# Merged prompt and decode attention: the new keys' scores two steps earlier, and the decode scores ahead of the prompt's scores on TensorE

## Chip, cores and metric

The kernel runs on one core of one Trainium2 chip. The metric is the device time of one execution in microseconds (us), the median of several runs.

## What is computed

One step of a hybrid causal decoder layer, for a prompt of 1024 tokens and for 8 decode sequences ("batches" below) of 8 tokens each, which have 4096 earlier tokens in a paged cache (32 pages of 128 tokens per batch). Of the layer only the differential attention matters here. There are 4 heads, each with two query/key sub-heads of 64 dims and a value of 128 dims; the rest of the layer (projections, gated linear attention, output projection, FFN, embedding) stands ahead of it and behind it.

```python
def diff_attend_prompt(q, k, v, lam):
    ...
        s = jnp.einsum('bqhcd,bkhcd->bhcqk', qi, k).astype(F32) * scale
        ...
        s = jnp.where(kpos[None, :] <= qpos[:, None], s, -jnp.inf)
        a = jax.nn.softmax(s, axis=-1)
        w = a[:, :, 0] - lam * a[:, :, 1]
        return jnp.einsum('bhqk,bkhv->bqhv', w.astype(v.dtype), v)
    ...

def diff_attend_sample(q, k, v, lam, k_past, v_past):
    ...
    s_past = jnp.einsum('bqhcd,bkhcd->bhcqk', q, k_past).astype(F32) * scale
    s_new = jnp.einsum('bqhcd,bkhcd->bhcqk', q, k).astype(F32) * scale
    s_new = jnp.where(jnp.tril(jnp.ones((T, T), dtype=bool)), s_new, -jnp.inf)
    a = jax.nn.softmax(jnp.concatenate([s_past, s_new], axis=-1), axis=-1)
    w = (a[:, :, 0] - lam * a[:, :, 1]).astype(v.dtype)
    return (jnp.einsum('bhqk,bkhv->bqhv', w[..., :P], v_past)
            + jnp.einsum('bhqk,bkhv->bqhv', w[..., P:], v))
```

## The kernel before, in words

`attention` (from line 1179) runs both attentions in one loop, written out by hand for each engine as a list of instructions with semaphore waits. The loop variable is t, with STEPS = 74 steps. Nothing reorders the lists: what stands first on an engine is issued first, and a wait holds everything behind it on that engine.

- Decode. A step t below NKV = 64 takes one group of 4 cache pages (512 past keys); NG = 8 groups make a batch. TensorE turns the keys of the 4 heads (`turn_keys`, L1425, 4 transposes a head), ScalarE copies heads 0 to 2 out of PSUM (`take_keys`, L1320), VectorE head 3 (L1588). One step later `score(t - 1)` (L1437) multiplies them with the batch's queries into the one bank S_BANK. VectorE takes the maximum (`max_scores`, L1593) and copies the scores to SBUF (`copy_scores`, L1599) in the step after that, and `score` waits for the copy of the scores before it (`s_taken`). LAG = 9 steps after its keys a group is exponentiated (`exps`, L1331, on ScalarE), its probabilities are turned (`turn_p`, L1460), copied by VectorE (`take_p`, L1627) and multiplied with the values (`values`, L1479).
- The end of a batch. `score_new` (L1447) gives the scores of the batch's 8 new tokens; `take_new` on VectorE adds their mask (L1609), takes their maximum (L1611), then the maximum over the batch (L1613) and its negative (L1615), on which the batch's exponentials wait. A second exponential (L1336) covers the new keys; its probabilities are turned by `turn_new_p` (L1454).
- Prompt. A unit is one head and one block of 128 queries, 32 units in the order of `UNITS` (1, 8, 2, 7, 3, 6, 4 and 5 blocks of keys, by turns), two steps each, one for each sub-head: `prompt_scores(t)` (L1389) on TensorE, then `prompt_maxima(t)` on VectorE (mask add L1548, maximum L1550, negative L1552), then the exponential on ScalarE in step t + 1 (`prompt_exps`, L1296). There is one pair of score banks, so `prompt_scores(t)` waits for the exponential of t - 1 (`exp_done`). In even steps VectorE also combines the two sub-heads of the unit before (`prompt_combine`, L1560 to L1565) ahead of the mask add; TensorE turns and multiplies the result (L1402, L1409).
- The ring. Turned keys, turned probabilities, the new keys' scores and the merged output of a batch share three PSUM banks in turn. `Ring` numbers the uses in TensorE's order, and `emptied(key)` waits until the use three places earlier has been copied away by its owner, ScalarE (`ring_act`) or VectorE (`ring_dve`).

SyncE loads the key pages, four steps ahead (a slot is free when its keys have been turned), and GpSimd the value pages, four steps ahead (free when `values` is done).

TensorE's order within a step is: turned keys 0 and 1; the prompt's product (even steps) or its turn (odd); turned keys 2 and 3; merge; turned new probabilities; turned probabilities; second part of the prompt's turn; `prompt_scores(t)`; `score(t - 1)`; `score_new`; `values`. VectorE's is: `finalize`, `max_scores(t - 2)`, `take_new`, `copy_scores(t - 2)`, `take_keys(t, 3)`, `take_new_p`, `take_p`, the combine, `prompt_maxima(t)`, the next batch's queries, `final_scale`. In the kernel before, `score_new` of batch b stands in step 8b + 8 and `take_new` in step 8b + 9.

Of the kernel before, what the change touches and what calls it, by code (L numbers as in the profile page):

```python
# [15 lines left out]
ALU = mybir.AluOpType  # L16
ACT = mybir.ActivationFunctionType
AX = mybir.AxisListType
# [5 lines left out]
DB, DS = 8, 8  # L24
# [1070 lines left out]
NG = NPG // 4  # L1095
NKV = DB * NG
LAG = NG + 1
STEPS = NKV + LAG + 1
UNITS = [(h, i) for h in range(H) for i in (0, 7, 1, 6, 2, 5, 3, 4)]
NU = len(UNITS)  # L1100
# [15 lines left out]
class Ring:  # L1116
# [4 lines left out]
    def __init__(self):  # L1121
        self.index, self.emptied, self.owners = {}, {}, []
        count = {"act": 0, "dve": 0}

        def use(key, owner):
            self.index[key] = len(self.owners)
            count[owner] += 1
            self.emptied[key] = count[owner]
            self.owners.append((owner, count[owner]))

        for t in range(STEPS):
            if t < NKV:
                for h in range(H):
                    use(("keys", t, h), "act" if h < 3 else "dve")
            b, last = divmod(t - LAG - NG, NG)
            if last == 0 and 0 <= b < DB:
                use(("merge", b), "act")
            v = t - LAG
            if 0 <= v < NKV:
                if v % NG == 0:  # L1140
                    use(("new_p", v // NG), "dve")
                use(("p", v), "dve")
            b, last = divmod(t - NG, NG)
            if last == 0 and 0 <= b < DB:
                use(("new_s", b), "dve")

# [32 lines left out]
def attention(nc, io, m, ps, scr, sems):  # L1179
# [14 lines left out]
    d = {n: sems("p4_" + n) for n in names.split()}  # L1194
# [36 lines left out]
    with nc.Block() as block:  # L1231
# [143 lines left out]
        def _(pe):  # L1375
            def prompt_scores(k):
                if k >= 2 * NU:
                    return
                n, c = divmod(k, 2)
                (h, i), u = UNITS[n], UNITS[n][0] % 2  # L1380
                if n % 8 == 0 and c == 0 and h:
                    pe.wait_ge(k_in[h], 64)
                if c == 0 and n >= QR:
                    pe.wait_ge(q_in[n % QR], 32 * (n // QR))
                if k:
                    pe.wait_ge(s["exp_done"], k)
                for r in range(2):
                    rows = slice(DK * r, DK * r + DK)
                    ins = pe.matmul(score_banks[:, r, 0:shown(i) * P], m.aq[rows, n % QR, c, :],  # L1389
                                    m.ak[u][rows, c, 0:shown(i) * P], start=True, stop=True)  # L1390
                ins.then_inc(s["scored"], 1)
# [99 lines left out]
            for t in range(STEPS):  # L1491
                v = t - LAG
                n, c = divmod(t, 2)
                if t < NKV:
                    turn_keys(t, 0)
                    turn_keys(t, 1)
                if c == 0 and 0 <= n - 2 < NU:
                    prompt_out(n - 2)
                if c == 1 and 0 <= n - 1 < NU:
                    prompt_turn(n - 1, 0)  # L1500
                if t < NKV:
                    turn_keys(t, 2)
                    turn_keys(t, 3)
                if t >= LAG + NG and (t - LAG - NG) % NG == 0:
                    merge((t - LAG - NG) // NG)
                if 0 <= v < NKV:
                    if v % NG == 0:
                        turn_new_p(v // NG)
                    turn_p(v)
                if c == 1 and 0 <= n - 1 < NU and pieces_of(n - 1) == 2:  # L1510
                    prompt_turn(n - 1, 1)
                prompt_scores(t)
                if 1 <= t <= NKV:
                    score(t - 1)
                if t and t % NG == 0 and t // NG <= DB:
                    score_new(t // NG - 1)
                if 0 <= v < NKV:
                    values(v)

        @block.vector  # L1520
        def _(dve):
# [68 lines left out]
            def max_scores(k):  # L1590
                b, g = divmod(k, NG)
                dve.wait_ge(d["s_full"], k + 1)
                dve.tensor_reduce(mx[:, g:g + 1], S_BANK, AX.X, ALU.max)  # L1593

            def copy_scores(k):
                b, g = divmod(k, NG)
                if b:
                    dve.wait_ge(d["exp_done"], k - NG + 1)
                dve.tensor_copy(m.ss[:, 512 * g:512 * g + 512], S_BANK).then_inc(d["s_taken"], 1)  # L1599

            def take_new(b):

                key = ("new_s", b)
                dve.wait_ge(d["ring_filled"], ring.filled(key))
                dst = m.ss[:, PAST:PAST + NS]
                if b:
                    dve.wait_ge(d["expn_done"], b)
                a = CONST_COLS["past"][0] + 56 - b * DS
                dve.tensor_tensor(dst, ring_bank(key)[:, 0:NS], m.consts[:, a:a + NS], ALU.add).then_inc(d["ring_dve"], 1)  # L1609
                dve.wait_ge(d["ring_dve"], ring.emptied[key])  # L1610
                dve.tensor_reduce(mx[:, NG:NG + 1], dst, AX.X, ALU.max).then_inc(d["mx"], 1)  # L1611
                dve.wait_ge(d["mx"], b * 2 + 1)
                dve.tensor_reduce(ssum[:, 1:2], mx, AX.X, ALU.max).then_inc(d["mx"], 1)  # L1613
                dve.wait_ge(d["mx"], b * 2 + 2)
                dve.tensor_scalar(negm[:, b % 2:b % 2 + 1], ssum[:, 1:2], -SC, None, ALU.mult).then_inc(d["negm"], 1)  # L1615

            def take_new_p(b):
# [31 lines left out]
            queries(0)  # L1649
            for t in range(STEPS):  # L1650
                v = t - LAG
                n, c = divmod(t, 2)
                if t >= LAG + NG and (t - LAG - NG) % NG == 0:
                    finalize((t - LAG - NG) // NG)
                if 0 <= t - 2 < NKV:
                    max_scores(t - 2)
                if 0 < t - 1 <= NKV and (t - 1) % NG == 0:
                    take_new((t - 1) // NG - 1)
                if 0 <= t - 2 < NKV:
                    copy_scores(t - 2)  # L1660
                if t < NKV:
                    take_keys(t, 3)
                if 0 <= v < NKV:
                    if v % NG == 0:
                        take_new_p(v // NG)
                    take_p(v)
                if c == 0 and 0 <= n - 1 < NU:
                    prompt_combine(n - 1)
                prompt_maxima(t)
                if t % NG == 4 and t // NG + 1 < DB:  # L1670
                    queries(t // NG + 1)
                if t >= LAG + NG - 1 and (t - LAG - NG + 1) % NG == 0:
                    final_scale((t - LAG - NG + 1) // NG)
                if HALVES < t <= HALVES + H:
                    norm_prompt(t - HALVES - 1)
# [890 lines left out]
```

## Time and profile before

| | |
|---|---|
| runs before | 2042.34, 2041.23, 2040.16 us; median 2041.23 |
| profiled execution | 2040.47 us, its span 2038.8 us |
| busy share of the span | PE 91%, PEld 84%, DVE 48%, ACT 30%, POOL 19% |
| mean granted TensorE clock | 0.963 |
| attention, by the trace | from 519 us (first turned keys) to about 945 us (last values) |

PE is TensorE's matmuls, PEld its weight loads, DVE is VectorE, ACT ScalarE, POOL GpSimd, SP SyncE. L1389 is line 1389 of the kernel before. Times in the trace count from the start of the span. A row of the timeline gives start, duration, engine, line, operation, what it writes and reads, the number of instructions and, in brackets, the engine's idle time ahead of it with what ended it. A row of the waits gives who waited for whom, the time in total, how many times, and the longest.

### The profile page before, as it was taken

To read this page: it belongs to the slowest core of one execution; us is meant where nothing else is said; L and a number is where in the kernel's file an instruction comes from. 1 tells how busy PE (TensorE), PEld (TensorE's weight loads), DVE (VectorE), ACT (ScalarE), POOL (GpSimd) and SP (SyncE) were. 2 spreads that over 40 slices of the span, in tenths; PEclk is the share of its full clock that TensorE was granted. 3 is DMA by queue.
4 is the path that set the end of the run, shared out by engine and by line. 5 is a ranking of instruction groups with operands and counts; after the bars stand their busy time and mean duration, and the time that the engine had idled before them with its cause. 6 is when DMAs were issued, how large, how long until landed. Compare 5 with 4: busy or idle time off the path is not lost. (4 is left out here: it accounts for less than half of the span.)

```text
span 2038.8 us, 35290 instructions
## 1 busy us (share of the span) xinstructions
PE 1863.9 (91%) x13412; PEld 1718.4 (84%) x13412; DVE 971.9 (48%) x1356; ACT 608.9 (30%) x1086; POOL 397.2 (19%) x393
## 2 busy tenths in 40 slices
PE   4999999575899999996999999999999999998898
PEld 4999999463566767664898999999999999998798
DVE  4223730486677777775325334344334333436443
ACT  4113321442465655563322211111111111113320
POOL 1112420232123333332112011101101110104110
PEclk9999999696899999998999999999999999999899
DMA  4332640204799999987111111111111111110221
GB/s 141 97 85 76 156 114 21 65 3 145 247 329 348 360 337 366 356 257 228 32 42 52 47 47 32 52 43 49 45 42 42 42 53 42 32 54 20 85 64 44
DMA packets 201583, 239.02 MB, mean 117 GB/s; under 512 B 15425, under 2 KB 142354, under 8 KB 201426
## 3 DMA queue, kind: packets, MB, share of 16 engines
q1 hardware_dynamic: 180946, 169.75, 27.0%
q0 software_dynamic: 20480, 67.13, 9.7%
q8 instruction: 105, 1.72, 0.4%
q14 instruction: 52, 0.43, 0.1%
HBM read 215.44 MB, written 16.91 MB: 114 GB/s over the span
## 5 line engine op out<-in xcount | busy, mean ns | idle before, releaser
L150 PE MATMUL psum<-h_hi,w_hi 128*128 128x364 f32 x1248 | 278.7, 332 | 2.8 <-issue 2.8
L150 PE MATMUL psum<-h_lo,w_hi 128*128 128x364 f32 x1248 | 276.3, 330 | 0.0
L150 PE MATMUL psum<-h_hi,w_lo 128*128 128x364 f32 x1248 | 275.2, 328 | 0.0
L2078 ACT ACTIVATE w_hi<-w_raw 128x1024 fp32r<-128x1024 f32 x66 | 68.8, 1059 | 586.3 <-PE psum L150 565.5
L150 PEld LDWEIGHTS psum<-h_hi,w_hi 128*128 128x128 f32 x1248 | 215.4, 189 | 4.9 <-issue 4.2
L150 PEld LDWEIGHTS psum<-h_lo,w_hi 128*128 128x128 f32 x1248 | 217.1, 189 | 0.0
L150 PEld LDWEIGHTS psum<-h_hi,w_lo 128*128 128x128 f32 x1248 | 216.7, 188 | 0.0
L2054 POOL TENSOR_TENSOR w_raw<-w_raw,gains 128x1024 f32<-128x1024 f32 x42 | 80.5, 1916 | 652.2 <-DMA w_raw<-in_w_ffn_gate 353.0
L1163 POOL DMA_DIRECT2D dec_v<-in_cache_v x256 | 137.5, 537 | 316.6 <-issue 316.6
L150 PE MATMUL psum<-x_hi,w_hi 128*128 128x364 f32 x792 | 188.5, 347 | 9.7 <-DVE x_lo L1911 5.8
L150 PE MATMUL psum<-x_hi,w_lo 128*128 128x364 f32 x792 | 176.5, 331 | 0.0
L150 PE MATMUL psum<-x_lo,w_hi 128*128 128x364 f32 x792 | 176.3, 331 | 0.0
L2194 DVE TENSOR_TENSOR h<-h,psum 128x1092 f32<-128x1092 f32 x88 | 113.5, 1289 | 108.0 <-PE psum L150 108.0
L150 PEld LDWEIGHTS psum<-x_hi,w_hi 128*128 128x128 f32 x792 | 137.3, 191 | 16.5 <-DVE x_lo L1911 6.3
L1425 PE MATMUL psum<-consts,dec_k 128*128 128x128 f32 x1024 | 139.7, 281 | 12.2 <-DVE dec_s L1609 6.1
L1320 ACT ACTIVATE dec_kt<-psum 128x512 f32<-128x512 f32 x192 | 108.4, 599 | 139.8 <-PE psum L1425 139.8
L1425 PEld LDWEIGHTS psum<-consts,dec_k 128*128 128x128 f32 x1024 | 115.2, 143 | 31.6 <-issue 17.0
L150 PEld LDWEIGHTS psum<-x_lo,w_hi 128*128 128x128 f32 x792 | 139.4, 190 | 0.0
L150 PEld LDWEIGHTS psum<-x_hi,w_lo 128*128 128x128 f32 x792 | 138.9, 190 | 0.0
L2173 DVE TENSOR_TENSOR t_up<-psum,rstd_and_sum 128x1092 f32<-128x1092 f32 x22 | 28.5, 1296 | 205.9 <-PE psum L150 205.9
L150 PE MATMUL psum<-hidden_hi,w_hi 128*128 128x364 f32 x528 | 116.9, 330 | 2.5 <-DVE w_lo L2164 2.5
L150 PE MATMUL psum<-hidden_lo,w_hi 128*128 128x364 f32 x528 | 117.4, 331 | 0.0
(262 smaller groups left out, 2793.4 us busy)
## 6 DMA issues: line engine op xcount, KB each, us to landing
dec_k<-in_cache_k SPq DMA_DIRECT2D x256, 256.0 KB, 5.1
dec_v<-in_cache_v POOLq DMA_DIRECT2D x256, 256.0 KB, 5.2
w_raw<-in_w_in SPq DMA_DIRECT2D x25, 512.0 KB, 3.9
w_raw<-in_w_ffn_gate SPq DMA_DIRECT2D x22, 512.0 KB, 3.9
w_raw<-in_w_ffn_up SPq DMA_DIRECT2D x22, 512.0 KB, 3.8
w_raw<-in_w_ffn_down SPq DMA_DIRECT2D x22, 512.0 KB, 3.6
feat_swap<-feat_n SPq DMA_DIRECT2D x32, 136.5 KB, 2.4
x_in<-in_x_prompt SPq DMA_DIRECT2D x4, 1024.0 KB, 8.2
```

The source lines that it names most:

```text
L150: ins = pe.matmul(out[:, c, 0:SPAN], w(k), x(k)[:, c * SPAN:c * SPAN + SPAN], start=n == 0 and w is whi and x is xhi, stop=n == len(ks) - ...
L1163: eng.dma_start(ring[:, slot, p:p + 1, :], cache[bass.ds(page, 1)].rearrange("o t f -> t o f")).then_inc(sem, 16)
L1320: act.activation(m.kt[:, t % 2, h, :], ring_bank(("keys", t, h)), ACT.Copy).then_inc(d["ring_act"], 1)
L1425: ins = pe.transpose(ring_bank(key)[:, p * P:p * P + P], m.kr[:, t % KR, p, h * P:h * P + P], ident)
L2054: gp.tensor_tensor(m.raw[:, u], m.raw[:, u], gain(m, "ffn").unsqueeze(2).broadcast_to([P, KT, P]), ALU.mult).then_inc(s["w_scaled"], 1)
L2078: act.activation(m.whi[:, slot], m.raw[:, u], ACT.Copy).then_inc(s["w_hi"], 1)
L2173: dve.tensor_tensor(spans(dst), dense[bank][:, :, 0:SPAN], spans(m.rb[:, :]), ALU.mult).then_inc(s["evacuated"], 1)
L2194: dve.tensor_tensor(spans(m.h[:, n]), spans(m.h[:, n]), dense[n % 2][:, :, 0:SPAN], ALU.add).then_inc(s["evacuated"], 1)
```

## The change

`score_new(b)` moves from step 8b + 8 to step 8b + 6 (`NEW_AT` = NG - 2), on TensorE and in the ring's numbering. On VectorE the mask add and the maximum of the new scores (`take_new`) move to step 8b + 7, behind `copy_scores`; the maximum over the batch and its negative become a function of their own, `batch_max`, which stays in step 8b + 9 between `max_scores` and `copy_scores`. And on TensorE, in every step, `score(t - 1)` stands ahead of `prompt_scores(t)`. No instruction is added or left out; the semaphore `mx` gets one more count per batch.

```diff
@@ constants and Ring
 LAG = NG + 1
+NEW_AT = NG - 2
...
-            b, last = divmod(t - NG, NG)
+            b, last = divmod(t - NEW_AT, NG)
             if last == 0 and 0 <= b < DB:
                 use(("new_s", b), "dve")
@@ TensorE
-                prompt_scores(t)
                 if 1 <= t <= NKV:
                     score(t - 1)
-                if t and t % NG == 0 and t // NG <= DB:
-                    score_new(t // NG - 1)
+                prompt_scores(t)
+                if t % NG == NEW_AT and t // NG < DB:
+                    score_new(t // NG)
                 if 0 <= v < NKV:
                     values(v)
@@ VectorE
-                dve.tensor_reduce(mx[:, g:g + 1], S_BANK, AX.X, ALU.max)
+                ins = dve.tensor_reduce(mx[:, g:g + 1], S_BANK, AX.X, ALU.max)
+                if g == NG - 1:
+                    ins.then_inc(d["mx"], 1)
...
                 dve.tensor_reduce(mx[:, NG:NG + 1], dst, AX.X, ALU.max).then_inc(d["mx"], 1)
-                dve.wait_ge(d["mx"], b * 2 + 1)
+
+            def batch_max(b):
+                dve.wait_ge(d["mx"], b * 3 + 2)
                 dve.tensor_reduce(ssum[:, 1:2], mx, AX.X, ALU.max).then_inc(d["mx"], 1)
-                dve.wait_ge(d["mx"], b * 2 + 2)
+                dve.wait_ge(d["mx"], b * 3 + 3)
                 dve.tensor_scalar(negm[:, b % 2:b % 2 + 1], ssum[:, 1:2], -SC, None, ALU.mult).then_inc(d["negm"], 1)
...
                 if 0 < t - 1 <= NKV and (t - 1) % NG == 0:
-                    take_new((t - 1) // NG - 1)
+                    batch_max((t - 1) // NG - 1)
                 if 0 <= t - 2 < NKV:
                     copy_scores(t - 2)
+                if (t - 1) % NG == NEW_AT and (t - 1) // NG < DB:
+                    take_new((t - 1) // NG)
                 if t < NKV:
                     take_keys(t, 3)
```

TensorE, from the turned probabilities of step 30 to those of step 31 (batch 3, so 8b + 6 and 8b + 7), before; `dec_p` are probabilities, `att_q` the prompt's queries, `dec_qb` the decode queries, `dec_k` the cache's keys:

```order
L1460 MATMUL psum<-consts,dec_p 128x128 x4
L1389 MATMUL psum<-att_k_97,att_q 128x384 x2
L1437 MATMUL psum<-dec_kt,dec_qb 32x512 x4
L1479 MATMUL psum<-dec_v,dec_pt 32x128 x16
L1425 MATMUL psum<-consts,dec_k 128x128 x8
L1402 MATMUL psum<-consts,att_p 128x128 x4
L1425 MATMUL psum<-consts,dec_k 128x128 x8
L1460 MATMUL psum<-consts,dec_p 128x128 x4
```

The same place in the changed kernel, whose lines stand one further on:

```order
L1461 MATMUL psum<-consts,dec_p 128x128 x4
L1438 MATMUL psum<-dec_kt,dec_qb 32x512 x4
L1390 MATMUL psum<-att_k_97,att_q 128x384 x2
L1448 MATMUL psum<-dec_new_k,dec_qb 32x64 x4
L1480 MATMUL psum<-dec_v,dec_pt 32x128 x16
L1426 MATMUL psum<-consts,dec_k 128x128 x8
L1403 MATMUL psum<-consts,att_p 128x128 x4
L1426 MATMUL psum<-consts,dec_k 128x128 x8
L1461 MATMUL psum<-consts,dec_p 128x128 x4
```

The decode scores and the prompt's scores have changed places, and the new keys' scores (`dec_new_k`) stand in this step. The second group of 8 `dec_k` transposes in step 31 begins with the third head; in the ring that head is now the third use after the new keys' scores.

VectorE in step 33 (8b + 9), from the end of the batch before to the copy of key head 3, before:

```order
L1644 TENSOR_SCALAR dec_osc<-psum,att_small 128x128
L1593 TENSOR_REDUCE att_small<-psum 128x1
L1609 TENSOR_TENSOR dec_s<-psum,consts 128x64
L1611 TENSOR_REDUCE att_small<-dec_s 128x1
L1613 TENSOR_REDUCE att_small<-att_small 128x1
L1615 TENSOR_SCALAR att_small<-att_small 128x1
L1599 COPY dec_s<-psum 128x512
L1588 COPY dec_kt<-psum 128x512
```

In the changed kernel the add on the new keys' scores and their maximum (there L1612 and L1614) stand in step 31 (8b + 7), from the maximum of the scores to the mask add of the prompt:

```order
L1594 TENSOR_REDUCE att_small<-psum 128x1
L1602 COPY dec_s<-psum 128x512
L1612 TENSOR_TENSOR dec_s<-psum,consts 128x64
L1614 TENSOR_REDUCE att_small<-dec_s 128x1
L1589 COPY dec_kt<-psum 128x512
L1632 COPY dec_pt<-psum 128x512
L1549 TENSOR_TENSOR psum<-psum,consts 128x2x128
```

They are behind the copy of the scores now; step 33 keeps the two instructions of `batch_max` between the maximum and the copy.

## Rows read from the trace of the kernel before

**Rows 1.** Windows, main stretch: length, busy time by engine, PEclk, DMA share, GB/s

```profile
600.00:650.00 50.00, 46.84 (x590) 35.14 (x589) 36.72 (x79) 29.94 (x79) 17.70 (x33) 1.00 1.03 350
```

**Rows 2.** Waits, 515 to 960 us: total, times, longest

```profile
DVE dec_kt L1588 <- PE psum L1425: 69.4, 46, 3.2
...
PE psum L1389 <- ACT att_p L1296: 11.6, 25, 1.0
...
PE psum L1425 <- DVE dec_s L1609: 6.1, 7, 1.0
...
ACT dec_p L1331 <- DVE att_small L1615: 2.6, 7, 0.9
```

**Rows 3.** Waits, 575 to 912 us, then 515 to 566 us

```profile
PE psum L1389 <- ACT att_p L1296: 7.9, 20, 0.6
...
PE psum L1389 <- ACT att_p L1296: 3.7, 5, 1.0
```

**Rows 4.** Windows, steps 3, 4, 5 and 7

```profile
536.41:541.56 5.15, 4.13 (x33) 2.29 (x29) 3.62 (x7) 2.83 (x6) 1.61 (x3) 1.00 1.05 344
541.56:545.90 4.34, 3.61 (x34) 2.41 (x30) 4.20 (x8) 3.27 (x8) 0.54 (x1) 1.00 1.06 336
545.90:550.23 4.33, 4.33 (x40) 3.04 (x36) 4.13 (x11) 3.00 (x7) 1.61 (x3) 1.00 1.05 345
...
555.97:561.22 5.25, 4.24 (x34) 2.40 (x30) 3.98 (x7) 2.94 (x6) 1.61 (x3) 1.00 1.04 366
```

**Rows 5.** Timeline, steps 3 and 4, TensorE and VectorE

```profile
540.57 1.07 PE L1437 MATMUL psum<-dec_kt,dec_qb 128*32 128x512 f32 x8
540.68 0.43 DVE L1548 TENSOR_TENSOR psum<-psum,consts 128x256 f32<-128x256 f32 x1 [1.47 <-PE psum L1389]
...
543.08 0.68 DVE L1599 COPY dec_s<-psum 128x512 f32<-128x512 f32 x1
```

**Rows 6.** Timeline, steps 30 and 31

```profile
701.40 0.92 PE L1389 MATMUL psum<-att_k,att_q 64*128 64x384 f32 x4
...
703.39 0.42 DVE L1548 TENSOR_TENSOR psum<-psum,consts 128x256 f32<-128x256 f32 x1
...
705.48 1.04 PE L1425 MATMUL psum<-consts,dec_k 128*128 128x128 f32 x8
705.51 0.68 DVE L1599 COPY dec_s<-psum 128x512 f32<-128x512 f32 x1
...
707.31 0.92 PE L1389 MATMUL psum<-att_k,att_q 64*128 64x384 f32 x4 [0.36 <-ACT att_p L1296]
```

**Rows 7.** Timeline, steps 22 and 23

```profile
650.98 1.13 PE L1389 MATMUL psum<-att_k,att_q 64*128 64x512 f32 x4
...
652.71 0.42 DVE L1548 TENSOR_TENSOR psum<-psum,consts 128x256 f32<-128x256 f32 x1
...
655.06 1.04 PE L1425 MATMUL psum<-consts,dec_k 128*128 128x128 f32 x8
655.09 0.68 DVE L1599 COPY dec_s<-psum 128x512 f32<-128x512 f32 x1
...
657.11 1.13 PE L1389 MATMUL psum<-att_k,att_q 64*128 64x512 f32 x4 [0.58 <-ACT att_p L1296]
```

**Rows 8.** Timeline, step 25 (8b + 9)

```profile
667.32 0.68 DVE L1593 TENSOR_REDUCE att_small<-psum 128x1 f32<-128x512 f32 x1
...
667.92 0.21 DVE L1609 TENSOR_TENSOR dec_s<-psum,consts 128x64 f32<-128x64 f32 x1
...
668.17 0.22 DVE L1611 TENSOR_REDUCE att_small<-dec_s 128x1 f32<-128x64 f32 x1
668.19 1.10 PE L1425 MATMUL psum<-consts,dec_k 128*128 128x128 f32 x8 [1.00 <-DVE dec_s L1609]
...
668.81 0.72 ACT L1331 ACTIVATE dec_p<-dec_s,att_small 128x512 f32<-128x512 f32 x1 [0.21 <-DVE att_small L1615]
...
670.58 0.30 PE L1454 MATMUL psum<-consts,dec_pn 128*128 128x128 f32 x1 [0.96 <-ACT dec_kt L1320]
```

## The prediction

> **What bounds the kernel now.** I read the page first, then the stretch in which the merged attention runs (about 519 to 945 us; nothing outside it is edited), by its windows, its waits and its order of time. In the main part of it TensorE is the bound: of 50 us it is busy 46.84, VectorE 36.72, ScalarE 29.94 [rows 1]. So what counts is TensorE's idle time, and only what the change takes away from it or adds to it. The waits of the stretch name two kinds that the change touches [rows 2]: TensorE's prompt scores waited 25 times for a prompt exponential, 11.6 us in all, and the third key head waited 7 times for a PSUM slot that VectorE frees with the add on the new keys' scores (L1609), 6.1 us. ScalarE waited 2.6 us in seven batch ends for the batch's negated maximum (L1615). VectorE itself waits for TensorE 46 times, 69.4 us, ahead of its key copy: that is the slack that hides small delays on it.
>
> I number a stretch's steps by the loop variable t; a batch b has steps 8b to 8b+7, and its first exponentials come in step 8b+9.
>
> **Part 1, decode scores ahead of the prompt's scores.** The instructions are the same, so only waits move. In steps 10 to 63 the old order lost 7.9 us in 20 waits [rows 3]. With the decode scores first, TensorE has about 1.0 us of work (L1437 lasts 1.07, the next group starts 1.0 after it, at 541.56 [rows 4, 5]) while the exponential ends; the longest of these waits is 0.6, so all of them go, provided that the decode scores' own input, VectorE's copy of the previous scores, is there. In step 31 this copy ended at 706.19 (705.51 + 0.68), while TensorE came to its prompt scores 0.36 ahead of 707.31, at 706.95 [rows 6]. It is there. Seven of the 20 waits lie in steps 8b+7, which part 2 prices: four of 0.36 as in step 31 [rows 6] and three of 0.58 as in step 23 [rows 7], 3.2 us. **Term 1: 7.9 - 3.2 = 4.7 us gained.** The prompt scores end 1.0 later in every step. VectorE's mask add follows the later of them and the combine of the odd unit: in step 30 scores ended at 702.32 and the mask add began at 703.39 [rows 6], so the delay is hidden; in step 22 they ended at 652.11, the mask add began at 652.71 [rows 7], so 0.44 of it comes through (652.11 + 1.0 + 0.05 - 652.71). In odd steps it comes through whole and is taken by the 69.4 us of slack.
>
> **Part 2, the new keys' scores two steps ahead.** They sit in a ring of three PSUM slots: whatever is the third entry after them waits for VectorE's add. Before, that was the third key head of step 8b+9; now it is the third key head of step 8b+7. VectorE's add is now behind the copy of the scores, not between maximum and copy. So I price the new wait from the old one: there the maximum ended at 668.00 (667.32 + 0.68), the add began 0.08 earlier, took 0.21, and TensorE went on at 668.19, that is 0.19 after the end of the instruction ahead of the add [rows 8]. In step 31 the copy ends at 706.19, so TensorE may go on at 706.38; it was there at 705.48 [rows 6]: 0.90 of new wait. In step 23 the copy ends at 655.77 (655.09 + 0.68), plus 0.44 from part 1, plus 0.19: 656.40 against 655.06 [rows 7]: 1.34. The 0.36 and 0.58 of the exponential that came behind it vanish inside it. Four steps of the first kind (15, 31, 47, 63), three of the second (23, 39, 55): 4 x 0.90 + 3 x 1.34 = 7.6, less 3.2. **Term 2: 4.4 us lost.** The trace of before does not show this wait. Its ends are none at all (the 3.2 would be gained) and the old wait of 1.00 [rows 8] plus 0.44 in all seven (10.1 - 3.2 = 6.9 lost); I keep the worked value, as it is made from rows of the same instructions.
>
> The old waits in steps 8b+9 go, 6.1 us, but nearly nothing is gained by that. Behind the third and fourth head TensorE waits again, 0.96 us, for ScalarE to copy the third head [rows 8], and ScalarE copies it only after the batch's first two exponentials, which start when the negated maximum is there. From the second key copy to that point ScalarE has no idle time except 0.21 [rows 8]. So TensorE comes 1.0 us earlier and waits 1.0 us longer. What is gained is what ScalarE gains: two VectorE instructions, 0.21 and 0.22 [rows 8], no longer lie ahead of the negated maximum, and of ScalarE's 2.6 us in seven waits [rows 2] about 0.3 each can go. **Term 3: 2.1 us gained** (ends 1.5 and 2.6). The four small matmuls move, they are not added.
>
> **Part 3, the steps ahead of the first values (2 to 8).** Here TensorE has little work: the four steps shown took 4.3 to 5.3 us [rows 4], and the old order lost 3.7 us in five waits for exponentials [rows 3]. With the new order the step becomes a closed loop through VectorE: mask add, reduction, decode maximum and copy, which took from 540.68 to 543.76 (543.08 + 0.68) [rows 5], 3.08; then about 0.06 to TensorE, decode scores 1.0, prompt scores 1.13 [rows 7], 0.05 back. That is 5.3 us for units of seven or eight blocks, where the old order ran the copy and the exponential side by side. Walking the loop step by step with these durations, step 3 takes 5.30 for 5.15, step 4 4.66 for 4.34, step 5 4.97 for 4.33, and step 7, with a new slot wait of 2.1 us, 6.28 for 5.25 [rows 4]; these four lose 2.1, the other three 0.4 together. **Term 4: 2.5 us lost**; ends: 3.7 gained, if all old waits simply go, and 3.7 lost, if each is replaced by one twice as long. The loop is made of rows of these very steps, so I take 2.5.
>
> **Sum:** -4.7 + 4.4 - 2.1 + 2.5 = +0.1 us. The profiled execution took 2040.47; the median of three is 2041.23, 0.76 above it. 2040.47 + 0.1 + 0.76 gives **2041.3 us**. Everything after the attention shifts with it and costs nothing. A measurement of this kernel tells about 0.2% (4.1 us) from no change, so the forecast is: no change. With the ends of the terms its own range is 2038 to 2044.5.
>
> **Transfers.** The main stretch moves 350 GB/s at a DMA share of 1.03 [rows 1], and a step of the early part 366 GB/s [rows 4]. So the transfers have been faster than the main stretch asks for, by 4%, and a gain of a few us in 340 asks for less than 1% more.
> The Trainium skill, "DMA: Bandwidth & Descriptors", section Specifications, gives about 358 GB/s as one core's limit to HBM; by it the main part would be at its end, and whatever the compute engines save would come back as waits for pages. The trace is against it in the one window of 366 GB/s.
>
> **Rivals.**
> A, faster: the slot of the new scores is free in time in steps 8b+7 (VectorE ahead by a microsecond). Then term 2 is a gain of 3.2, and without the wait in step 7 the early loss is 1.4: -4.7 - 3.2 - 2.1 + 1.4 = -8.6, 2032.6 us. Against it: the copy ended 0.7 after TensorE was there in both steps shown [rows 6, 7]. It needs VectorE to come a full 0.9 earlier.
> B, slower: the decode scores' 1.0 us lands whole on VectorE ahead of all seven slot waits. It decides at the point where the mask add of step 8b+6 starts with the prompt scores and not with the combine; in step 30 they would end at 703.3 and the mask add began at 703.39 [rows 6], a margin of under 0.1. If the combine came 1.0 earlier than there, each wait would be 1.9: 7 x 1.9 - 3.2 = 10.1 in place of 4.4, 2047.0 us. Against it: nothing in the change makes the combine earlier.
> C, the transfers are at their limit: terms 1 to 3 (2.4 gained) come back as waits for pages and term 4 stays, 2043.7 us. For it: the share of 1.03 [rows 1]; against it the 366 GB/s, and that no wait for a key page stands among the waits of the stretch. The rule cited above is this case.
>
> **Chances.** Forecast 0.78; A 0.08; B 0.06; C 0.08. A and B lie outside the range, C inside; with a little of the forecast's ends left out I give 2037.5 to 2045.0. Faster by over 0.2%: A and a little, 0.09. Slower by over 0.2%: B and a little, 0.07. Within: 0.84.
>
> **What would show it.** Right, if in the profile after: prompt scores wait for exponentials hardly at all; the third key head waits 0.9 to 1.4 us for the add on the new scores in steps 15, 23, 31 and so on, and about 2 in step 7; the turn of the new probabilities (L1454) waits about 1.6 in place of 0.96; steps 3 to 8 are longer, the decode scores waiting there for the copy. Wrong, if the add's wait is absent (A), if it is near 2 everywhere (B), if key turns wait for DMA (C), or if decode scores wait for the copy in the main part.

## Result: slower by 8 us, and where the time went

The changed kernel took 2048.46 us (median of five runs, 2047.73 to 2052.1) where the kernel before took 2040.37 (median of five in the same session, 2036.58 to 2042.34): a ratio of 1.0045, 95% interval 1.0033 to 1.0058. That is slower by more than 0.2%. The forecast, 2041.3 us and no change, was wrong, and the time lies above the range.

The waits of the changed kernel from 515 to 960 us (total, times, longest), to be read against [rows 2]:

```profile
PE psum L1455 <- ACT dec_kt L1321: 11.0, 6, 2.0
...
PE psum L1426 <- DVE dec_s L1612: 6.6, 8, 1.8
...
PE psum L1438 <- DVE dec_s L1602: 4.8, 6, 1.3
...
ACT dec_p L1332 <- DVE att_small L1620: 0.4, 1, 0.4
```

Line numbers have moved by one to five: L1390 is the prompt scores, L1426 the key turns, L1438 the decode scores, L1455 the turn of the new probabilities, L1480 the values, L1488 the merge; on VectorE L1602 is the copy of the decode scores and L1612 the add on the new scores. Most of what was foreseen is there. No wait of the prompt scores' matmuls for an exponential is left among these waits (11.6 us in 25 before [rows 2]), ScalarE's wait for the negated maximum is 0.4 in place of 2.6 [rows 2], and the wait for the add on the new scores stands at 6.6 us in its new place. The decode scores wait for the copy, 4.8 us, in five early steps as foreseen and once in the last, and the turned new probabilities wait 11.0 us in six batch ends (0.96 each before [rows 8]). TensorE's waits alone come out about even: -11.6 + 0.5 + 4.8 + 5.2. The lengths of the steps tell another story. Windows of the kernel before (length, busy time by engine, granted clock, DMA share, GB/s): step 6; steps 2 to 8; steps 9 to 62; step 63 to the last values; steps 25 and 29 alone:

```profile
550.23:555.97 5.74, 5.74 (x48) 3.98 (x45) 3.29 (x10) 2.74 (x8) 0.54 (x1) 1.00 1.05 341
...
532.08:565.98 33.90, 30.25 (x241) 19.21 (x238) 27.08 (x54) 20.08 (x48) 6.44 (x12) 1.00 1.03 339
565.98:904.44 338.46, 317.79 (x3957) 236.11 (x3951) 251.14 (x532) 203.50 (x522) 113.72 (x212) 1.00 1.00 342
904.44:945.38 40.94, 27.11 (x446) 19.77 (x442) 23.89 (x41) 14.03 (x39) 18.77 (x30) 0.95 0.71 217
665.67:674.32 8.65, 6.70 (x87) 4.75 (x83) 7.00 (x20) 5.21 (x14) 2.15 (x4) 1.00 1.04 374
692.24:697.73 5.49, 5.49 (x75) 4.20 (x71) 5.26 (x13) 3.70 (x9) 2.14 (x4) 1.00 1.03 380
```

The same of the changed kernel, without step 6, and with a stretch inside step 25 at the end:

```profile
533.29:570.04 36.75, 30.61 (x240) 19.22 (x238) 27.73 (x58) 20.55 (x48) 6.46 (x12) 1.00 1.03 331
570.04:915.67 345.63, 328.46 (x3961) 232.31 (x3960) 251.79 (x531) 203.53 (x522) 114.06 (x212) 0.99 0.98 333
915.67:954.79 39.12, 25.52 (x438) 18.40 (x434) 23.59 (x41) 13.94 (x39) 18.81 (x30) 1.00 0.73 224
670.57:680.76 10.19, 8.18 (x87) 5.25 (x83) 5.95 (x16) 5.21 (x14) 2.15 (x4) 0.83 1.04 370
698.66:704.29 5.63, 5.63 (x74) 4.09 (x71) 4.49 (x11) 3.71 (x9) 2.15 (x4) 1.00 1.00 375
...
675.70:679.10 3.40, 3.40 (x17) 1.41 (x17) 0.93 (x2) 1.34 (x4) 0.15 (x1) 0.50 1.05 356
```

Steps 2 to 8 are 2.85 us longer, steps 9 to 62 are 7.17 longer. (The last part is 1.82 shorter; the clock of the kernel before was low there once, 0.95 in its row, and with the order alone, at 1.00, the part took 39.05 too. The remaining -0.2 of the 8.0 between the spans lies in stretches that the change doesn't touch.) In the main part two things stand that no wait shows. Step 29 has no idle time of TensorE in either kernel (its busy time is its length), and yet it takes 5.63 for 5.49. And step 25 takes 10.19 for 8.65, at a mean granted clock of 0.83: for 3.4 us in it the clock is 0.50, that is 1.2 GHz in place of 2.4.

**The first: 0.14 us in a step.** TensorE in step 29, start, length and operation, before:

```profile
695.22 0.70 PE L1389 MATMUL psum<-att_k,att_q 64*128 64x256 f32 x4
695.86 1.07 PE L1437 MATMUL psum<-dec_kt,dec_qb 128*32 128x512 f32 x8
696.74 1.06 PE L1479 MATMUL psum<-dec_v,dec_pt 128*32 128x128 f32 x32
```

and after:

```profile
701.65 1.06 PE L1438 MATMUL psum<-dec_kt,dec_qb 128*32 128x512 f32 x8
702.65 0.70 PE L1390 MATMUL psum<-att_k,att_q 64*128 64x256 f32 x4
703.28 1.08 PE L1480 MATMUL psum<-dec_v,dec_pt 128*32 128x128 f32 x32
```

The decode scores last the same, but what follows them starts 0.88 us after their start where it is the values (695.86 to 696.74), and 1.00 after where it is the prompt scores (701.65 to 702.65). Decode scores and values use the array in the same shape, 128 rows by 32 columns; prompt scores use 64 by 128. The prompt scores' own successor starts 0.64 and 0.63 after them. So the group behind the decode scores can begin 0.12 earlier if it has their shape, and the change has put one of another shape between. The next step's keys begin 0.99 after the start of the values before, and 1.01 after the change; with that the 0.14 is nearly whole. The weight loads of the same two groups (PEld), the values before and the prompt scores after, show where the 0.12 lies:

```profile
696.31 0.13 PEld L1479 LDWEIGHTS psum<-dec_v,dec_pt 128*32 128x32 f32 x4 [0.30 <-DVE dec_pt L1627]
...
702.64 0.30 PEld L1390 LDWEIGHTS psum<-att_k,att_q 64*128 64x128 f32 x4 [0.84 <-issue]
```

The first weights of the values were loaded from 0.43 ahead of their first matmul, while the decode scores still ran; those of the prompt scores only as their matmul began. So it is in all of steps 9 to 62: 0.88 behind all 54 decode scores of the kernel before, 0.99 or 1.00 behind all 54 with the order alone, and where TensorE didn't wait, a group with the shape of the one ahead of it had its weights loaded 0.03 to 0.43 early in either of these two, a group with another shape never. No run changes the shape and nothing else. The Trainium skill, "TensorEngine Tiling (Array Packing)", section Tiling Modes (Key Properties), says that changing the tiling mode drains TensorE, while a change of tile alone doesn't. The rows agree with that: before, a step with values changes shape three times (keys to prompt scores, to decode scores, back to keys), after it four times.

**The second: the clock.** TensorE, then ScalarE, in step 25 of the changed kernel, to be read against [rows 8]:

```profile
675.31 0.30 PE L1455 MATMUL psum<-consts,dec_pn 128*128 128x128 f32 x1 [2.01 <-ACT dec_kt L1321]
...
676.90 1.94 PE L1438 MATMUL psum<-dec_kt,dec_qb 128*32 128x512 f32 x8
...
673.54 0.72 ACT L1332 ACTIVATE dec_p<-dec_s,att_small 128x512 f32<-128x512 f32 x1
...
674.60 0.57 ACT L1321 ACTIVATE dec_kt<-psum 128x512 f32<-128x512 f32 x1
```

Before, TensorE's idle time at this batch end came in two pieces, 1.00 ahead of the third key head and 0.96 ahead of the turned new probabilities, with 1.4 us of work between them [rows 8]. The first piece is gone with the slot wait, and, since ScalarE copies the third head no earlier than its exponentials allow, the second has grown to 2.01. So far this is what the prediction says. But right behind this piece the granted clock falls (at 0.50 from 675.7): the decode scores take 1.94 in place of 1.07 [rows 5]. It falls in the same way in steps 41 and 57, not in 9, 17, 33 and 49, whose pieces are 1.61 to 1.68.

### The profile page after: what moved, and what is told of

Same layout as the page of the kernel before. It is cut to its first block and busy times, and to the rows that moved or that the text cites. A ratio compares the mean times of both kernels' runs of the same rounds, so it can differ in the third digit from the quotient of the medians.

```text
span 2046.8 us, 35290 instructions
## 1 busy us (share of the span) xinstructions
PE 1872.5 (91%) x13412; PEld 1713.7 (84%) x13412; DVE 973.5 (48%) x1356; ACT 609.3 (30%) x1086; POOL 397.5 (19%) x393
## 5 line engine op out<-in xcount | busy, mean ns | idle before, releaser
L1426 PE MATMUL psum<-consts,dec_k 128*128 128x128 f32 x1024 | 139.7, 281 | 12.9 <-DVE dec_s L1612 6.6
L1426 PEld LDWEIGHTS psum<-consts,dec_k 128*128 128x128 f32 x1024 | 115.2, 143 | 29.4 <-issue 13.5
```

The lines of the kernel that those rows point to most:

```text
L1426: ins = pe.transpose(ring_bank(key)[:, p * P:p * P + P], m.kr[:, t % KR, p, h * P:h * P + P], ident)
```

## Experiments

Eleven kernels were run, each 5 to 12 times beside the kernel before (its medians in the three sessions: 2040.39, 2038.67 and 2039.84). Each has one profile, of one of these runs; what is said of idle pieces and of the clock is said of that execution.

**The two parts apart.** The first kernel is the one before with the order of the change and nothing else:

```diff
-                prompt_scores(t)
                 if 1 <= t <= NKV:
                     score(t - 1)
+                prompt_scores(t)
                 if t and t % NG == 0 and t // NG <= DB:
                     score_new(t // NG - 1)
```

> Only the decode scores ahead of the prompt's scores; the new keys' scores stay where they were. Theory (three separate causes: lost overlap, clock, slot wait): TensorE loses 0.14 us in each of the 55 steps that have values, since the prompt's scores now stand between decode scores and values (+7.7); the waits for exponentials go in the main part (-7.9); steps 2 to 8 lose about 1.9 without the slot wait in step 7; the idle time at batch ends stays in two pieces of 1 us, so the granted clock stays at its upper level there. Sum +1.7 on 2040.4: 2042. Rival (all of the loss is the new slot wait): order alone gains the 7.9 and loses 1.9: 2034. Rival (all of the loss is the order): 2048.

Measured: 2039.32 us, ratio 0.9997 (0.9988 to 1.0006). Windows of step 6, steps 9 to 62 and step 29:

```profile
552.31:558.04 5.73, 5.73 (x46) 3.97 (x44) 3.67 (x9) 2.74 (x8) 0.54 (x1) 1.00 1.05 330
...
568.66:905.50 336.84, 323.82 (x3957) 230.40 (x3952) 252.18 (x533) 203.51 (x522) 113.73 (x212) 1.00 1.00 343
...
694.38:700.01 5.63, 5.63 (x75) 4.09 (x71) 4.49 (x11) 3.70 (x9) 2.14 (x4) 1.00 1.03 377
```

Step 29 takes 5.63 here too, so the 0.14 belongs to the order. Step 6, which has no values and in which keys follow the decode scores in the old order, takes 5.73 for 5.74: no loss where one shape change is only exchanged for another. In 54 steps (9 to 62) 0.14 makes 7.6 us; the whole of these steps is 1.62 shorter, so the exponentials' waits were worth about 9.2 (an estimate from these two numbers), where their rows say 7.9 [rows 3]: a wait of 0.36 in its row was worth 0.43 of its step. That is part of why the kernel came out 2.7 below the 2042 that its own sum gave; neither rival came. The order alone gains in the main part nearly the 2.0 that it loses in steps 2 to 8.

The second kernel is the changed one with the old order:

```diff
+                prompt_scores(t)
                 if 1 <= t <= NKV:
                     score(t - 1)
-                prompt_scores(t)
```

> Only the new keys' scores two steps ahead; the prompt's scores stay ahead of the decode scores. Theory (three causes): no 0.14 per step; the third key head waits about 0.85 in steps 8b+7 in place of 0.36 or 0.58 for the exponential (+2.8); batch ends -0.3 each (-2.1); TensorE idle there in one piece of 1.6 to 2.0 us. Without a lower clock after it 2041; if the granted clock falls after some of these pieces, 1.8 us more for each, up to 2047 for three. Rival (all is the slot wait): 2048 without any low clock in the batch-end steps. Rival (all is the order): 2040.

Measured: 2046.33 us, ratio 1.0035 (1.0023 to 1.0046). The order alone costs nothing in sum; the move alone costs 5.9 of the 8 us. Its windows of step 25:

```profile
668.57:678.50 9.93, 8.03 (x87) 5.69 (x83) 6.87 (x19) 5.15 (x14) 2.15 (x4) 0.83 1.05 377
```

It has the low clock as the changed kernel has it, in steps 9, 17, 25, 41 and 49, each time behind one idle piece of 1.6 to 1.9 us.

**Is it the idle piece?** The third kernel is the changed one, with the merge's matmul, which stands just ahead of the idle piece, issued five times into the same place:

```diff
-                pe.matmul(ring_bank(("merge", b))[0:32, 0:DV], const(m, "merge"), m.osc[:, :], start=True, stop=True
-                          ).then_inc(d["ring_filled"], 1)
+                for again in range(5):
+                    ins = pe.matmul(ring_bank(("merge", b))[0:32, 0:DV], const(m, "merge"), m.osc[:, :],
+                                    start=True, stop=True)
+                ins.then_inc(d["ring_filled"], 1)
```

> The changed kernel with the small merge product issued five times instead of once into the same place (batch ends 1 to 7), so that TensorE's one idle piece of 2.0 us there is cut to about 1. Theory (clock): the granted clock no longer falls in steps 25, 41, 57, which go from 10.2 back to about 8.3 us: -5.6 on 2048.5, so 2043. Rival (the batch end is longer because of VectorE's or ScalarE's chain): steps 25, 41, 57 keep 10.2 us, 2048.5 or a little more.

Measured: 2043.07 us, ratio 1.0013 (1.0003 to 1.0023). Windows of steps 9 to 62 and of step 25:

```profile
569.66:910.60 340.94, 328.97 (x4009) 235.78 (x4007) 251.88 (x531) 203.30 (x522) 113.74 (x212) 1.00 0.99 338
...
670.19:678.81 8.62, 7.48 (x95) 5.54 (x91) 5.96 (x16) 5.20 (x14) 2.15 (x4) 1.00 1.05 370
```

More work, and the kernel is 5.4 us faster than the changed one: from step 17 on the pieces are 0.8 and 1.1 us now, the clock stays at 1.00 in all these steps, and step 25 takes 8.62 for 10.19. Steps 9 to 62 are 4.69 shorter, 1.56 for each of the three falls.

**What does the slot wait cost?** The fourth kernel is the changed one with the add on the new scores as VectorE's first work of its step, ahead of the decode maximum and copy:

```diff
+                if t and (t - 1) % NG == NEW_AT and (t - 1) // NG < DB:
+                    take_new((t - 1) // NG)
                 if 0 <= t - 2 < NKV:
                     max_scores(t - 2)
...
-                if (t - 1) % NG == NEW_AT and (t - 1) // NG < DB:
-                    take_new((t - 1) // NG)
```

> The changed kernel with VectorE's add and maximum on the new keys' scores as the first work of step 8b+7, ahead of maximum and copy of the decode scores. Theory (slot wait): the add ends before TensorE comes to the third key head, so the waits of 0.48 (steps 15, 31, 47, 63) and 0.94 (23, 39, 55) there go to under 0.2, and most of the 1.8 in step 7: -5, so 2043.5, if the granted clock falls as often as in the changed kernel. Rival (the third head is held by something else, or the time comes back at the decode scores): 2048.5.

Measured: 2039.1 us, ratio 1.0001 (0.9991 to 1.0012). In the changed kernel the add had stood here, in step 23 (VectorE's copy and add, then TensorE's third head):

```profile
659.75 0.68 DVE L1602 COPY dec_s<-psum 128x512 f32<-128x512 f32 x1
660.35 0.21 DVE L1612 TENSOR_TENSOR dec_s<-psum,consts 128x64 f32<-128x64 f32 x1
...
660.62 1.09 PE L1426 MATMUL psum<-consts,dec_k 128*128 128x128 f32 x8 [0.94 <-DVE dec_s L1612]
```

Windows of the new kernel, steps 9 to 62, 23 and 25, and TensorE in step 25:

```profile
566.27:901.91 335.64, 322.73 (x3961) 230.73 (x3959) 251.72 (x531) 203.56 (x522) 114.07 (x212) 1.00 1.01 345
...
653.89:659.58 5.69, 5.69 (x71) 3.68 (x67) 4.46 (x10) 3.64 (x8) 2.15 (x4) 1.00 1.04 366
665.00:673.70 8.70, 6.70 (x87) 4.68 (x83) 5.95 (x16) 5.21 (x14) 2.15 (x4) 1.00 1.04 376
...
669.74 0.30 PE L1455 MATMUL psum<-consts,dec_pn 128*128 128x128 f32 x1 [2.00 <-ACT dec_kt L1321]
```

Step 23 has no idle time left; it took 1.09 more in the changed kernel (658.36 to 665.14, 6.78), step 31 took 0.71 more (6.33 for 5.62). So the six slot waits of steps 9 to 62 cost some 5.4 us. The surprise is step 25: the idle piece ahead of the turned new probabilities is 2.00 us here as well, and the clock did not fall in any step of the main part of this profile. Three falls of 1.56 would be 4.7, about what the median came out below the 2043.5 expected; but the profile is the fastest of the eleven runs, and whether the others had no fall either isn't shown.

**Is the fall then due to the slot wait?** In the profiles so far, either cure had been enough. The fifth kernel is the second with the fourth's edit: the move alone, without its slot wait.

```diff
+                prompt_scores(t)
                 if 1 <= t <= NKV:
                     score(t - 1)
-                prompt_scores(t)
...
+                if t and (t - 1) % NG == NEW_AT and (t - 1) // NG < DB:
+                    take_new((t - 1) // NG)
                 if 0 <= t - 2 < NKV:
                     max_scores(t - 2)
```

> The new scores two steps ahead, their add first on VectorE, and the prompt scores ahead of the decode scores as before: the move alone without its slot wait. Theory (in the runs so far the clock fell behind a batch end only where a slot wait stood two steps ahead of it; the move is worth about 0.3 us at each of seven batch ends): no fall in the main stretch, 2037 to 2039 us. Rival (TensorE's one idle piece of 1.6 to 1.9 us is enough by itself, as in the run of the move alone with its slot wait): falls of 3.4 us behind several batch ends, 2042 to 2046 us.

Measured: 2044.62 us, ratio 1.0023 (1.0015 to 1.0032). The theory is out, the rival holds. (The profiled run was the fastest of twelve, 2039.61, by what lies ahead of the attention; from step 2 to the last values it took 418.6 us, the kernel before 413.3.) TensorE in steps 33 and 57:

```profile
717.57 0.30 PE L1455 MATMUL psum<-consts,dec_pn 128*128 128x128 f32 x1 [1.82 <-ACT dec_kt L1321]
...
719.18 1.93 PE L1438 MATMUL psum<-dec_kt,dec_qb 128*32 128x512 f32 x8
...
871.83 0.30 PE L1455 MATMUL psum<-consts,dec_pn 128*128 128x128 f32 x1 [1.90 <-ACT dec_kt L1321]
...
873.48 1.06 PE L1438 MATMUL psum<-dec_kt,dec_qb 128*32 128x512 f32 x8
```

There is no slot wait in the main part, and the clock fell in steps 17, 25, 33, 41 and 49, behind pieces of 1.81 to 1.90; behind the 1.90 of step 57 it did not.

**Does the length decide, or the moment?** Two more kernels. In the sixth, which is the third with two issues in place of five, the pieces are a little shorter than in the changed kernel:

```diff
-                for again in range(5):
+                for again in range(2):
```

> The changed kernel with the merge's matmul issued twice, the second with the same result in the same place. Theory (the length of the idle piece decides: in the changed kernel it fell behind 2.0 us and not behind 1.68 us): the pieces of steps 25, 41 and 57 come to 1.8 us; if that is short enough, no fall, 2043 us. Rival (the length is not what decides, the move alone had falls behind 1.6 to 1.9 us): three falls as in the changed kernel, 2048 us.

In the seventh, the changed kernel does some 1.7 us more work once, in step 13 (7.37 us there for 5.63), and is the same otherwise:

```diff
-                for p in range(4):
+                for p in list(range(4)) * (5 if v == 4 else 1):
                     ins = pe.transpose(ring_bank(("p", v))[:, p * P:p * P + P], m.pg[:, v % 2, p * P:p * P + P], ident)
```

> The changed kernel with the four turns of step 13 issued five times into the same place: 1.76 us more work of TensorE, once, and every later step that much later; nothing else differs. Theory (each idle piece of 2.0 us makes the clock fall, whenever it comes): again three falls, in steps 25, 41 and 57, 2050 us. Rival (it depends also on the moment at which the piece comes): the falls move to other batch ends, or one goes; 2045 to 2050 us.

Measured: 2049.45 (1.0046, 1.0031 to 1.006) and 2052.23 (1.0065, 1.0052 to 1.0078). TensorE in step 25 of the sixth kernel:

```profile
677.33 0.30 PE L1455 MATMUL psum<-consts,dec_pn 128*128 128x128 f32 x1 [1.78 <-ACT dec_kt L1321]
...
678.59 1.94 PE L1438 MATMUL psum<-dec_kt,dec_qb 128*32 128x512 f32 x8
```

and in steps 25 and 41 of the seventh:

```profile
675.87 0.30 PE L1455 MATMUL psum<-consts,dec_pn 128*128 128x128 f32 x1 [2.01 <-ACT dec_kt L1321]
...
676.88 1.07 PE L1438 MATMUL psum<-dec_kt,dec_qb 128*32 128x512 f32 x8
...
776.72 0.30 PE L1455 MATMUL psum<-consts,dec_pn 128*128 128x128 f32 x1 [2.00 <-ACT dec_kt L1321]
...
778.26 1.93 PE L1438 MATMUL psum<-dec_kt,dec_qb 128*32 128x512 f32 x8
```

1.78 us made the clock fall as 2.0 did, in steps 25, 41 and 57. In the seventh kernel the very piece that brought a fall in the changed kernel (2.01, step 25) brought none, and the same piece in steps 41 and 57 did. So the length alone doesn't decide. Over all profiles 1.61 (step 9) brought a fall in three of seven, 1.67 to 1.68 in none of nine pieces. Two falls more came in steps 7 and 9 of both kernels, which the changed kernel's profile doesn't have. Step 7 of the seventh kernel (6.21 us at 1.00 in the changed kernel):

```profile
554.44:562.29 7.85, 6.04 (x37) 2.63 (x31) 3.91 (x8) 3.05 (x6) 1.61 (x3) 0.78 0.99 340
```

These steps stand ahead of its edit: up to step 12 it is the changed kernel, instruction for instruction. So the same pieces in the same code brought a fall in one execution and none in another, and the fall that step 25 lost need not be due to the added work. The moment at which a piece comes is what is left of the two ideas, but no run sets it alone: what decides stays open. Both medians lie above what either idea gave (2048 and 2050 at most), which the two falls more would explain.

**Filling the idle piece.** If the piece is the trouble, work that is there anyway can be put into it. In the step of a batch's first values the turned probabilities are moved behind the prompt scores, first in the kernel before, then in the changed kernel (where the prompt scores already stand behind the decode scores):

```diff
-                if 0 <= v < NKV:
-                    if v % NG == 0:
-                        turn_new_p(v // NG)
+                first_group = 0 <= v < NKV and v % NG == 0
+                if 0 <= v < NKV and not first_group:
                     turn_p(v)
...
                 prompt_scores(t)
+                if first_group:
+                    turn_new_p(v // NG)
+                    turn_p(v)
```

> The kernel before, in which the first step of a batch's values turns the new exponentials and the first old ones behind the prompt scores. Theory (TensorE's idle time at the seven batch ends, 0.96 us ahead of the turned new exponentials, is a wait that other work can fill): the rows of that wait vanish, about 0.9 us x 7 = 6 us less, 2034 us, if nothing is late behind it. Rival (the turned exponentials still have to be copied before the values start, with only the 1.0 us of the decode scores between them): the wait moves to the values, 2038 to 2041 us.

> The changed kernel with the same late turns. Theory (the granted clock falls because TensorE's idle time at a batch end stands in one piece of 2.0 us): with the piece filled by prompt turns and scores the clock does not fall behind steps 25, 41 and 57 (3 x 1.8 = 5.4 us less) and up to 1 us of idle time goes in each of seven steps: 2036 to 2043 us. Rival (the fall comes from the slot wait two steps ahead, not from the idle piece): the clock still falls in those steps, 2043 to 2048 us.

Measured: 2030.23 us, ratio 0.9958 (0.9945 to 0.9971), and 2036.7 us, ratio 0.9991 (0.998 to 1.0001). TensorE in step 25 of the first, and its steps 9 to 62:

```profile
667.41 1.10 PE L1425 MATMUL psum<-consts,dec_k 128*128 128x128 f32 x8 [1.00 <-DVE dec_s L1611]
...
669.89 0.33 PE L1454 MATMUL psum<-consts,dec_pn 128*128 128x128 f32 x1
```

```profile
566.64:900.01 333.37, 318.58 (x3959) 236.12 (x3952) 250.80 (x532) 202.71 (x522) 113.71 (x212) 1.00 1.01 348
```

The wait of 0.96 ahead of the turned new probabilities is gone without a new one behind it in this step. Steps 9 to 62 are 5.1 us shorter than in the kernel before; the medians differ by 8.4, and the profile, of the slowest of the five runs, doesn't show the rest. In the changed kernel the 2.0 us piece becomes two of about 0.4, and no fall is left in steps 2 to 62:

```profile
668.69 1.06 PE L1438 MATMUL psum<-dec_kt,dec_qb 128*32 128x512 f32 x8 [0.47 <-DVE dec_s L1604]
...
671.87 1.08 PE L1480 MATMUL psum<-dec_v,dec_pt 128*32 128x128 f32 x32 [0.41 <-DVE dec_pt L1634]
```

**All of it.** The last two kernels take the new scores early, their add first on VectorE, the late turns, and the old order of the prompt scores; the second puts the decode scores first in the six steps of sixteen where the wait for the exponential was longest:

```diff
+                ahead = t > NG and t % 16 in (3, 4, 7, 8, 11, 15)
+                if ahead and t <= NKV:
+                    score(t - 1)
                 prompt_scores(t)
...
-                if 1 <= t <= NKV:
+                if 1 <= t <= NKV and not ahead:
                     score(t - 1)
```

> New scores early, their rows taken first on VectorE, prompt scores ahead of decode scores as before, late turns at a batch end. Theory (the parts add up: the lost 0.14 us per step is not paid, the slot wait is gone, the exponentials' waits are back, the idle piece is partly filled): 2032 to 2036 us. Rival (the prompt scores' waits for the exponentials come back in full and the late turns only move the wait): 2039 to 2041 us.

> As b1_best, but from step 9 on the decode scores stand ahead of the prompt scores in the six steps of sixteen whose prompt scores wait for an exponential by more than 0.14 us. Theory (a step pays 0.14 us where the decode scores stand first, and saves the wait where there is one): some 9 us of waits gone for 21 x 0.14 = 3 us lost, 5 to 6 us below b1_best. Rival (the waits come from work that falls behind elsewhere, and come back in the next step): as b1_best within 1 us.

Measured: 2029.07 us, ratio 0.9948 (0.9936 to 0.9961), and 2027.91 us, ratio 0.9948 (0.9935 to 0.996). Both beat both kernels, the first by more than was expected. Steps 9 to 62 of the first:

```profile
565.96:897.45 331.49, 317.42 (x3964) 236.35 (x3960) 250.48 (x531) 202.77 (x522) 114.08 (x212) 1.00 1.01 350
```

and of the second, where the choice takes only 2 of the expected 5 to 6 us off them, and TensorE at the start of step 41, where time came back:

```profile
566.16:895.66 329.50, 320.36 (x3964) 235.74 (x3960) 250.29 (x531) 202.79 (x522) 113.73 (x212) 0.99 1.02 352
```

```profile
761.28 1.97 PE L1426 MATMUL psum<-consts,dec_k 128*128 128x128 f32 x8 [2.72 <-DMA dec_k<-in_cache_k]
```

The steps with the decode scores first are each shorter by about the wait less 0.14, as the theory says, 5.8 us without steps 40 and 41; but ahead of step 41 a key page is late by 2.72 us, and the clock falls with that piece too (0.81 in step 41): these two steps are 3.8 longer. One profile can't tell whether this belongs to the kernel. The intervals of the two don't separate them. Nor do they separate either from the late turns alone, which take the most part of the gain with the smallest edit. Steps 9 to 62 of the second moved 352 GB/s.

## Why the prediction was wrong

The sum was +0.1 us (and 0.76 to the median); the spans differ by 8.0. Term by term, for the same stretches:

- **The step that failed: "The instructions are the same, so only waits move."** They are the same, but the spacing between two of them depends on which follow each other. The decode scores' successor starts 0.88 after them if it has their shape and 1.00 if not; in all, 0.14 a step, 7.6 us in steps 9 to 62 (an estimate from the steps without idle time). The number was in the prediction: "the next group starts 1.0 after it" was read from step 3 [rows 5], where key turns follow, and carried to steps where values follow, which the rows of step 29 put at 0.88. The run with the order alone shows a loss of 0.14 in each step with values that has no idle time in either kernel, and none in step 6.
- **Term 1**, 4.7 us gained (7.9 with the seven steps that part 2 prices): right in kind and a little small. With the order alone the main part is shorter by 1.62 in spite of the 7.6, so the waits were worth about 9.2; their rows leave some 0.07 of each wait out.
- **Term 2**, 4.4 us lost: the mechanism was right (L1612 is what the third head waits for, in the steps named), the size too large. TensorE's idle time in step 23 is 0.94 and not 1.34. VectorE's copy ended at 660.43 (659.75 + 0.68), 2.07 after the start of the step, where the sum had 1.86 + 0.44; so half of the 0.44 that part 1 added didn't come. By the step's length the wait costs 1.09, and 0.71 in step 31; the prediction had 1.34 and 0.90. In all six of steps 9 to 62 it is 5.4 us by the run with the add first, where the prediction had 6.7.
- **Term 3**, 2.1 us gained: half right, and here lies the second failure. "TensorE comes 1.0 us earlier and waits 1.0 us longer" is what the trace shows (2.01 ahead of L1455, ScalarE's wait 0.4 in place of 2.6), and steps in which the clock stayed are about 0.3 shorter (step 33 took 8.21 before, and 7.86 after), all but step 9. But the sum put the price of making one idle piece out of two at nothing, and gave no reason: three falls of the granted clock followed, 4.7 us by the run with the merge issued five times.
- **Term 4**, 2.5 us lost: right, 2.85, and right step by step: steps 3, 4, 5 and 7 lost 2.1 together, as foreseen (5.40, 4.75, 4.85 and 6.21 us). The loop through VectorE was walked with rows of its own steps.

For steps 9 to 62: 7.6 (shape) - 9.2 (exponentials) + 5.4 (slot) + 4.7 (clock) leaves 8.5; 7.17 was measured, and the remaining 1.3 is about what the batch ends gain where the clock stayed. The prediction had -2.4 for these terms. Rival A did not come (the add's wait is there), nor B (it is 0.94 and not 1.9). Rival C did not come either: no key page is waited for in the changed kernel. It shows in faster ones: key pages were late ahead of step 7 by 0.77 with the late turns alone and by 1.24 and 0.80 in the last two, and ahead of step 41 in the last, whose main part moved 352 GB/s. By the Trainium skill, "DMA: Bandwidth & Descriptors", section Specifications, about 358 GB/s would be the limit; a mean of 352 with late pages is close to what that rule says, and windows such as step 29 of the kernel before, 380 GB/s, are above it.

Of the chances, 0.78 lay on a sum without either of the two costs that decided, and the rivals differ from it in waits alone. Both costs were outside the waits. Taken off the measured 2048.46 one by one, either leaves a time inside the range (2040.9 without the 7.6, 2043.8 without the 4.7): with one of them alone the range would have held by luck.

## What to carry to other kernels

When groups of matmuls change places, compare the spacing of each pair that becomes neighbours, from rows of the same pair, and not the durations: a group between two of the same array shape takes an overlap away that no wait shows. When an edit removes one of two waits whose common cause lies further down, count the idle time that is left and ask whether it now stands in one piece; here that brought the clock down in some executions and steps, and the same time in two pieces, or filled with work that was due anyway, did not in any profile. What paid most, some 8 us by the medians, was to move work that had no need to wait (the prompt scores) ahead of work that had to.

## What was not expected of the hardware

- The granted clock fell to 0.50 for 3.4 us, and cost about 1.6 us each time, behind single idle pieces of TensorE of 1.61 (step 9 of the seventh kernel), 1.78, 1.9 and 2.0 us. The same pieces of 1.9 and 2.0 us brought no fall in other steps and other runs (2.00 in step 25 of the kernel with the add first; 2.01 in step 25 of the shifted one), and 1.61 brought one in step 9 of the seventh kernel and none in the changed one, whose code is the same up to there. In the profiles where the batch ends had two pieces of about 1 us, or one of at most 1.5, it stayed at 1.00 there.
- More work made the kernel faster: four more matmuls at each batch end took 5.4 us off the changed kernel.
- The decode scores' successor starts 0.12 us earlier if it has their array shape (0.88 for 1.00), its weights loaded 0.43 ahead of it, with nothing in TensorE's idle times to show it.
